# Mixture-of-experts stage: blocks of 64 rows in column halves become blocks of 32 rows in column quarters

## The reference, cut to what matters

```python
def routed_experts(x, expert_ids, gates, wg, wu, wd):
    # assignments sorted by expert, each expert's segment padded to whole blocks
    ...
    def run_block(args):
        tok, gate, e = args
        xb = x_pad[tok]
        hdn = jax.nn.silu(xb @ wg[e]) * (xb @ wu[e])
        return (hdn @ wd[e]) * gate[:, None]
    ...
```

## Time and profile before

| what | value |
|---|---|
| median of 3 runs | 3208.79 us (3207.67 to 3209.72) |
| the profiled execution | 3201.68 us, span 3199.9 us |
| preparation of the experts, 2104 to 2152 | 48 us |
| loop over 82 blocks, 2152 to 3110 | 958 us, 11.66 us per block |
| wait for the last store, 3110 to 3118.3 | 8.3 us |
| tail, 3118.3 to 3200 | 81.7 us |

### The profile page before, as it was taken

The page is one execution under the profiler, slowest core; times in us unless marked ns, Lnnn a source line. Parts: engine busy times, 40 slices in busy tenths (PEclk is TensorE's granted clock), DMA queues, the critical chain, the costliest instruction groups (busy, mean ns, idle before and its releaser), DMA issues. The chain is left out here.

```text
span 3199.9 us, 68748 instructions
## 1 busy us (share of the span) xinstructions
PE 2931.1 (92%) x28939; PEld 1726.0 (54%) x28940; DVE 1408.7 (44%) x3430; ACT 974.0 (30%) x1872; POOL 174.9 (5%) x256
## 2 busy tenths in 40 slices
PE   6988999999999488988898799949999999999988
PEld 2432455454554378878887455535555555555543
DVE  2245356665666545656666344541221211212117
ACT  2357234343344323333333121202122222212215
POOL 0000000000000000000001000001111000111104
PEclk8999999999999799999999799969999999999999
DMA  7541123232233496665552743455896568667758
GB/s 271 208 136 56 50 93 118 93 126 85 100 126 115 132 226 176 179 172 154 154 165 83 233 149 130 165 138 210 306 339 222 180 237 330 253 229 266 261 191 335
DMA packets 373260, 575.69 MB, mean 180 GB/s; under 512 B 31263, under 2 KB 230999, under 8 KB 369977
## 3 DMA queue, kind: packets, MB, share of 16 engines
q1 hardware_dynamic: 332888, 470.13, 43.7%
q0 software_dynamic: 18080, 72.10, 6.4%
q10 hardware_dynamic: 22080, 30.36, 3.3%
HBM read 426.97 MB, written 145.54 MB: 179 GB/s over the span
## 5 line engine op out<-in xcount | busy, mean ns | idle before, releaser
L451 PE MATMUL pj_P<-pj_hT,pj_wc 128*128 128x448 f32 (+2 forms) x1600 | 590.4, 516 | 0.9 <-ACT pj_stage L579 0.9
L2503 PE MATMUL moe_PG<-wgu,moe_xT 128*64 128x256 f32 x5248 | 582.2, 380 | 0.7 <-ACT moe_xT L2401 0.7
L2503 PEld LDWEIGHTS moe_PG<-wgu,moe_xT 128*64 128x64 f32 x5248 | 377.6, 137 | 226.0 <-issue 47.6
L451 PEld LDWEIGHTS pj_P<-pj_hT,pj_wc 128*128 128x128 f32 x1600 | 294.1, 189 | 256.5 <-issue 239.4
L2510 PE MATMUL moe_PTY<-wd,moe_hT 128*64 128x512 f32 x1312 | 317.7, 603 | 0.0
L2404 ACT ACT_TABLE_LOAD x82 | 105.2, 1283 | 496.9 <-issue 496.8
L1984 PE MATMUL merge_PO<-merge_w,merge_mT 128*128 128x512 f32 x544 | 238.5, 596 | 0.0
L2363 DVE TENSOR_TENSOR moe_sg<-moe_sg,moe_PG 128x128 f32<-128x128 f32 x164 | 46.3, 282 | 296.5 <-ACT moe_sg L2404 296.5
L1984 PEld LDWEIGHTS merge_PO<-merge_w,merge_mT 128*128 128x128 f32 x544 | 102.4, 191 | 123.1 <-issue 122.4
L2367 DVE COPY moe_hT<-moe_PH 128x128 f32<-128x128 f32 x164 | 47.9, 292 | 267.2 <-PE moe_PH L2495 267.2
L2370 DVE COPY moe_y<-moe_PTY 128x512 f32<-128x512 f32 x82 | 56.7, 692 | 208.3 <-PE moe_PTY L2510 208.3
(11 more groups left out here) (385 smaller groups left out, 4133.4 us busy)
## 6 DMA issues: line engine op xcount, KB each, us to landing
wgu<-in_w_gate SPq DMA_DIRECT2D x32, 2048.0 KB, 9.4
wgu<-in_w_up SPq DMA_DIRECT2D x32, 2048.0 KB, 15.0
wd<-in_w_down SPq DMA_DIRECT2D x32, 2048.0 KB, 16.6
re_hkf<-scratch_hk SPq DMA_DIRECT2D x60, 640.0 KB, 8.1
re_rkf<-scratch_rk SPq DMA_DIRECT2D x68, 320.0 KB, 6.9
scratch_hk<-pj_hk SPq DMA_DIRECT2D x16, 1344.0 KB, 5.8
scratch_y_rows<-moe_y ACTq DMA_DIRECT2D x164, 128.0 KB, 5.2
scratch_rk<-pj_rk SPq DMA_DIRECT2D x16, 1120.0 KB, 4.4
```

Of the source, the lines that this page charges most:

```text
L451: ins = eng.matmul(bank[:, 0:wp], wc[:, j, k, :], hT[:, k, k0:k0 + wp], start=(k == 0), stop=(k == KD - 1), skip_group_check=True)
L2503: ins = eng.matmul(PG[64 * c:64 * c + 64, j, 0:256].rearrange("p (a b) -> p a b", a=2), x_rows, wgu[p][:, :, k, o:o + 128], start=(k == 0) ...
```

## The change

- `BLOCK` is 32. An expert has at least two blocks. The block's rows are gathered as four quarters of 1 KB into `xg[p]` [128, 256] (two buffers); POOL copies `xg[p]` to `xc`, from which PE makes two transposes instead of four.
- gate_up uses four column quarters of the array, 32 stationary columns each: 32 matmuls of 256 columns. down uses four quarters as well: 16 matmuls of 256 columns.
- PE's order in a step g is `turn(g + 1)`, `turn_hid(g - 1)`, `gate_up(g)`, `down(g)`, and `down(g)` computes the result of block g - 1. It needs `hT_kept >= g` and `y_kept >= g + 1`.
- In DVE's iteration g the copy to `y` (`keep_y(g + 1)`) stands ahead of the copy to `hT`. It waits for `down(g)` and for `y_out`, that is, for the landing of the store of the step before.
- The stores move from the ACT queue to SP's, four DMAs of 32 KB, in a loop per expert, between the loads of weights: at the end of an expert gate and up of the expert after next are issued; then, in the next expert, first one store, then w_down, then the other stores.
- ACT preloads the sigmoid's table once, ahead of the loop.
- Zeros are stored to all of `y_rows` in `merge`, three DMAs of 512 KB per tile on SP's queue; ACT's loop of such stores is gone, and results are stored one block further down.
- In the preparation two scans replace the 17 additions of `carry`, and the block map has 201 columns instead of 101.
- The loads of `maps` come after the last store of a result, since that is now ahead of them on SP.

```diff
-BLOCK = 64
-MAX_BLOCKS = T * TOP_K // BLOCK + N_EXPERTS
+BLOCK = 32
+MIN_BLOCKS = 2
+MAX_BLOCKS = T * TOP_K // BLOCK + MIN_BLOCKS * N_EXPERTS
...
(merge, SP, after the store of h2)
+                for part in range(3):
+                    eng.dma_start(t["y_rows"][ds(at_tile(i, n) * 3 + 128 * part, 128), :], zeros[:, :]).then_inc(ev("zeros_out"), 16)
...
(experts, SP)
-                def load_pair(i):
-                    before, first, second = blocks_of_pair(eng, i - 1)
-                    for p in range(2):
-                        done = before + first if p == 0 else before + first + second
-                        eng.wait_ge(ev("gu_made"), done)
-                        load_expert(eng, t, i * 2 + p, wgu[p], wd[p], loaded[p], range(2))
-                        eng.wait_ge(ev("y_made"), done)
-                        load_expert(eng, t, i * 2 + p, wgu[p], wd[p], loaded[p], range(2, 3))
+                def store_y(g):
+                    eng.wait_ge(ev("y_kept"), g + 2)
+                    ...
+                    for n in range(4):
+                        eng.dma_start(t["y_rows"][ds(at * BLOCK, BLOCK), 256 * n:256 * n + 256], y[32 * n:32 * n + 32, :]).then_inc(ev("y_out"), 16)
+                def expert_blocks(g0, count, down_of, gate_up_of):
+                    store_y(g0)
+                    if down_of is not None:
+                        e, p = down_of
+                        load_expert(eng, t, e, wgu[p], wd[p], loaded[p], range(2, 3))
+                    with eng.Fori(1, count) as b:
+                        store_y(g0 + b)
+                    if gate_up_of is not None:
+                        e, p = gate_up_of
+                        eng.wait_ge(ev("gu_made"), g0 + count)
+                        load_expert(eng, t, e, wgu[p], wd[p], loaded[p], range(2))
+                def pair(i):
+                    before, first, second = blocks_of_pair(eng, i)
+                    expert_blocks(before, first, (i * 2 + 1, 1), (i * 2 + 2, 0))
+                    expert_blocks(before + first, second, (i * 2 + 2, 0), (i * 2 + 3, 1))
...
+                store_y(total(eng))
                 eng.wait_ge(ev("rows_made"), 1)
                 eng.dma_start(maps[:, 0, :], ...
...
(experts, DVE)
-                for n in range(NT):
-                    src = ...
-                    step(eng.tensor_tensor(carry[:, n + 1, :], carry[:, n, :], src, ALU.add))
+                    step(eng.tensor_tensor_scan(carry[:, experts_of, :]..., restart[:, experts_of, :]..., PTY[:, h, 0:n], 0.0, ALU.mult, ALU.add))
...
+                def keep_y(g):
+                    eng.wait_ge(ev("y_made"), g)
+                    eng.wait_ge(ev("y_out"), g * 64)
                     eng.tensor_copy(y[:, :], PY[:, :]).then_inc(ev("y_kept"), 1)
+                with eng.Fori(0, n_blocks) as g:
+                    eng.wait_ge(ev("sigmoid_made"), g + 1)
+                    eng.tensor_tensor(sg[:, :], sg[:, :], PG[:, 0, 0:128], ALU.mult).then_inc(ev("silu_made"), 1)
+                    eng.wait_ge(ev("silu_made"), g + 1)
+                    eng.tensor_tensor(hid[:, :], sg[:, :], PG[:, 0, 128:256], ALU.mult).then_inc(ev("hid_ready"), 1)
+                    keep_y(g + 1)
+                    eng.wait_ge(ev("h_turned"), g + 1)
+                    eng.tensor_copy(hT[:, :], PH[:, 0, 0:128]).then_inc(ev("hT_kept"), 1)
...
(experts, ACT)
+                eng.preload_act_table_set("sigmoid_and_others")
-                with eng.Fori(total(eng), MAX_BLOCKS + 1) as g:
-                    eng.dma_start(t["y_rows"][ds(g * BLOCK, BLOCK), :], zeros[:, :]).then_inc(ev("row_blocks"), 16)
-                    for n in range(2):
-                        eng.dma_start(t["y_rows"][ds(g * BLOCK, BLOCK), 512 * n:512 * n + 512], y[64 * n:64 * n + 64, :]).then_inc(ev("y_out"), 16)
...
(experts, POOL)
+                        eng.tensor_copy(row[:, p:p + 1], rows[:, ds(i * 2 + (p + 2), 1)]).then_inc(ev("row_ready"), 1)
+                        eng.wait_ge(ev("x_turned"), i * 2 + (p + 1))
+                        eng.tensor_copy(xc[:, :], xg[p][:, :]).then_inc(ev("x_moved"), 1)
+                        ...
+                        gather(p)
...
(experts, PE)
+                def gate_up(g, p):
+                    eng.wait_ge(ev("xT_kept"), g + 1)
                     for k in range(KD):
+                        x_rows = xT[:, k % 2, 32 * (k // 2):32 * (k // 2) + 32]
+                        for q in range(4):
+                            ins = eng.matmul(PG[32 * q:32 * q + 32, 0, 0:256].rearrange("p (a b) -> p a b", a=2), x_rows, wgu[p][:, :, k, 128 * q:128 * q + 128],
                                              start=(k == 0), stop=(k == KD - 1))
+                def down(g, p):
+                    eng.wait_ge(ev("hT_kept"), g)
+                    eng.wait_ge(ev("y_kept"), g + 1)
+                    for k in range(KE):
+                        for n in range(4):
+                            ins = eng.matmul(PY[32 * n:32 * n + 32, :], hT[:, 32 * k:32 * k + 32], wd[p][:, k, 256 * n:256 * n + 256],
+                                             start=(k == 0), stop=(k == KE - 1))
+                def rest_of_expert(g0, count, p):
+                    with eng.Fori(1, count) as b:
+                        g = g0 + b
+                        turn(g + 1)
+                        turn_hid(g - 1)
+                        gate_up(g, p)
+                        down(g, p)
```

More of the change, by code:

```diff
@@ L2211, in experts @@
         x1 = sb("x1", [128, N_KEPT, D])
[L2212 to L2219, removed]
+        quarter = sb("quarter", [128, 1])
+        restart = sb("restart", [128, N_EXPERTS, NT])
+        xg = [sb(f"xg{p}", [128, 256]) for p in range(2)]
+        xc = sb("xc", [128, 256])
+        xT = sb("xT", [128, 2, 128])
+        sg = sb("sg", [128, 128])
+        hid = sb("hid", [128, 128])
+        hT = sb("hT", [128, 128])
+        y = sb("y", [128, 256])
         PTY = ctx.enter_context(nc.psum_tensor("moe_PTY", [128, 2, 512], F32))
@@ L2266, in _ @@
                 with eng.Fori(1, 1 + N_KEPT) as i:
-                    load_pair(i)
+                    pair(i)
                     eng.dma_start(x1[:, ds(i - 1, 1), :].rearrange("p a n -> p (a n)"), t["x1"][ds(i * 128 - 128, 128), :]).then_inc(ev("x1_in"), 16)
-                with eng.Fori(1 + N_KEPT, N_EXPERTS // 2) as i:
-                    load_pair(i)
+                with eng.Fori(1 + N_KEPT, N_EXPERTS // 2 - 1) as i:
+                    pair(i)
+                before, first, second = blocks_of_pair(eng, N_EXPERTS // 2 - 1)
@@ L2271, in _ @@
+                expert_blocks(before, first, (N_EXPERTS - 1, 1), None)
+                expert_blocks(before + first, second, None, None)
+                store_y(total(eng))
                 eng.wait_ge(ev("rows_made"), 1)
@@ L2497, in gate_up, with turn, turn_hid @@
-                def gate_up(p, j):
+                def turn(g, first=False):
+                    eng.wait_ge(ev("x_moved"), g + 1)
+                    if not first:
+                        eng.wait_ge(ev("xT_kept"), g)
+                    for k in range(2):
+                        ins = eng.transpose(PT[:, k, :], xc[:, 128 * k:128 * k + 128], ident)
+                    ins.then_inc(ev("x_turned"), 1)
+                def turn_hid(g):
+                    eng.wait_ge(ev("hid_ready"), g + 1)
+                    eng.transpose(PH[:, 0, 0:128], hid[:, :], ident).then_inc(ev("h_turned"), 1)
@@ L2504, in gate_up @@
                                              start=(k == 0), stop=(k == KD - 1))
-                    ins.then_inc(ev("g_made" if j == 0 else "gu_made"), 1)
-                def down(p, j, c):
-                    for n in range(2):
-                        ins = eng.matmul(PY[64 * n:64 * n + 64, :], hT[:, j, 64 * c:64 * c + 64], wd[p][:, 2 * c + j, 512 * n:512 * n + 512],
-                                         start=(j == 0 and c == 0), stop=(j == 1 and c == 1))
-                    return ins
@@ new lines, in rest_of_expert, with next_expert @@
+                def rest_of_expert(g0, count, p):
[5 more added lines that the diff above has]
+                        down(g, p)
+                        eng.nop()
+                def next_expert(g, i, p):
+                    turn(g + 1)
+                    turn_hid(g - 1)
+                    for matrix in range(2):
+                        eng.wait_ge(loaded[p][matrix], i * 16 + 16)
+                    eng.sem_inc(ev("expert_begun"), 1)
+                    gate_up(g, p)
+                    down(g, 1 - p)
+                    eng.wait_ge(loaded[p][2], i * 16 + 16)
+                    eng.sem_inc(ev("down_begun"), 1)
@@ new lines, in _ @@
+                turn(0, first=True)
+                before, first, second = blocks_of_pair(eng, 0)
+                for matrix in range(3):
+                    eng.wait_ge(loaded[0][matrix], 16)
+                eng.wait_ge(ev("xT_kept"), 1)
+                turn(1)
+                gate_up(before, 0)
```

(9 more changed lines are left out.)

169 lines of the change are left out of this document (80 added, 89 removed).

## The result

The changed kernel takes 3323.17 us (median of four runs, 3316.77 to 3329.83), beside 3209.26 us for the kernel before on the same chip: a ratio of 1.035, interval 1.033 to 1.037. The forecast was 3262, with a range up to 3320. The direction was right, and the loss is twice as large as forecast.

A forecast was written before the change was run, and what follows sets the result against it. PE was taken to bound the loop: 885 of work, 94 of store stalls and 27 of clock make 1006 (+48); with +5 outside the loop, 3255 us profiled, 3262 in the median's scale. Range 3150 to 3320.

The forecast's parts named there:

- PE bounds the loop, a step is near half, the blocks are 150: Loop: PE's step falls from 11.66 to 5.89 us, 82 blocks become 150; 885 us, 73 less than 958.
- Stores go to the end of SP's queue and PE waits in the third step of every expert: Expert boundaries: the store lands behind gate and up at D + 17.1 (D: last down's end), so PE's down waits; 0.72.
- The size of the wait: Loop: PE stalls 2.1 us at a plain boundary, longer with x1 or handed-on lateness; 94 us over 30 boundaries.
- the same walk: Going through the 30 expert boundaries with the row counts: 14 stalls of 2.1, 11 of about 3.5, four of 5.0, one of 6.4.
- The clock: Loop: PE's granted clock falls after idle time, 1.7 us lost at each of 16 stalls of 3.4 us and more; 27 us.
- upper cases: Loop, more waits than forecast: the table load stays (+22) and loads pass at 380 GB/s (+33), 3317 us; chance 0.05.
- Not held up, 3141: Rival, loop: stores pass queued loads or loads finish in time, no stall or clock loss, -68 us; chance 0.11.
- Quarters in series, 3970: Rival, PE's matmuls: the column quarters don't run side by side, a step of 11.1 us, about +710; chance 0.01.
- Parts forecast at nothing: ACT's table load gone, POOL's copy hidden, weights never late, zeros in merge 0 (up to +5 at the last tile).

The follow-up runs named there:

- Experiment 1: The changed kernel with its four y stores per block issued on ACT's queue instead of SP's: 3211.3 us, 1.002 of the kernel before.
- experiment 6: The changed kernel with the load of w_up moved behind the store of the next expert's first step, ahead of w_down: 3340.37 us, 1.041 of the kernel before.
- experiment 9: The changed kernel with weight loads on ACT's queue, stores alone on SP's, x1 ahead of the loop: 3179.11 us with one y tile, then (last kernel) 3129.99 with two.
- 4: The changed kernel with the twelve x1 tiles loaded ahead of the loop, on SP's queue behind the constants: 3303.36 us, 1.032 of the kernel before.

## Why the prediction was right or wrong

- **PE bounds the loop, a step is near half, the blocks are 150.** Right: 5.80 us against 5.89, 13 us better over the loop. The quarters run side by side.
- **Stores go to the end of SP's queue and PE waits in the third step of every expert.** Right, all 30. Experiment 1 took the waits away by the queue, experiment 6 moved them by the order in the queue. With x1 ahead in both, separate queues gave 3179 against 3303 (experiments 9 and 4), 124 us (what SP gains in not issuing loads is in it). The Trainium skill (DMA: Bandwidth & Descriptors, section "Issuing engines are not separate DMA queues") says that starting DMAs from several engines only saves issuing time; these runs differ from it, and the prediction was right not to follow it. That section also says that the DMAs of all engines interleave on the same 16 DMA engines. The trace agrees as far as a store on its own queue still took 6.3 us under the loads, and 47 us hang on that.
- **The size of the wait: 94 forecast, 139 measured by the same walk** (134.8 in the view of waits). This is the step that failed by most microseconds. At a plain boundary the walk has 3.5 us (3.35 in the view) against 2.1. Three terms make the difference. Gate left at D + 3.5 and not D + 3.1. PE was ready at D + 15.6 and not D + 15.9, since its steps were shorter. And the passage of the bytes was met to a tenth (gate and up through 13.7 us after gate's issue, the store 14.05), but DVE's copy began only 0.8 to 1.0 us after the store's last packet, at every boundary, where I had put 0.1: the time from a last packet to its landing was missing from the sum. With x1 the view has 5.4 against a forecast of 3.4. There SP is held 4.23 us in issuing x1 and the store of G is issued only at D + 10.6, but that isn't what made it late. In all twelve its first packet ran 14.2 to 14.8 us after gate's issue, at least 7.1 after its own, and without x1 12.9 to 13.2 after gate's. So x1's place in the queue costs 1.4 us, as forecast, and the store's own packets are under way for 1.8 us instead of some 1.2.
- **The clock: 27 forecast, some 53 to 58 measured.** This is the step that failed most for its size. I charged 1.7 us to the 16 waits of 3.4 us and more, from a single row of 2.25 us idle. Nearly every wait turned out at 3.2 or more, and 28 brought the half clock, at about 2 us each; two of 3.38 and 3.41 us did not. The 58 are what is left of 197 beside the 139; some 5 of them are small gaps, since the last kernel of experiment 9, without waits or falls, has an excess of 5. Of -13 for the steps, +45 for the waits and +31 for the clock the sum is +63, which is the loop's error (1069.6 against 1006).
- **The range.** Its upper cases were taken one at a time. A longer passage lengthens the wait and lets more waits reach the clock, so the two errors go together; 3317 to 3320 had no room for that.
- **Not held up, 3141.** Even off the loads' queue one y tile gives 3179 (experiment 9): a landing of 5.2 to 6.8 us was harmless beside a step of 11.66 and is not beside 5.80. That rival was priced too low by this.
- **Quarters in series, 3970.** The sum of this rival is off: its 710 are over the kernel before, and were added to 3262, which holds the waits already. It should have been some 3930. Nothing else hangs on it.
- **Parts forecast at nothing.** Right: with the zeros PE is busy for 268.91 us of the 280 in merge (267.37 in the earlier trace rows), the DMA share is up from 0.48 to 0.70, and merge's own length grows by 0.4 us; no table load is left in the loop; POOL's copy is waited for only ahead of the first block; no expert's weights come late. From merge's last matmul to the first gate_up it is 54.0 us against 51.8, +2.2 where the forecast had some +4; the tail is +1.6 against +1.5. The 3.0 us ahead of merge belong to no term of the sum.

## What to carry to other kernels

When a change shortens a step, set every hand-off's landing time against the new step, not against its bytes: the same queue that cost nothing at 11.66 us per step cost 112 to 124 us at 5.80. Keep small stores with a waiter off the queue of the bulk loads, and give their tile a second buffer; here, with x1 moved in all three, the first alone left 52 us of 198, the second alone 23, both together 5. Add to a DMA's passage the time from its last packet to its landing, here 0.8 us. Of 30 idle stretches of PE of 3.2 to 6.5 us, 28 cost about 2 us of clock on top of their length.

## What the runs showed of the hardware that was not expected

- One store DMA of 128 KB in four pieces landed later (8.9 us) than four of 32 KB (6.3), with 132 packets for 192, and with at most 4 of them under way at once instead of up to 9. Fewer issues are not fewer microseconds.
- Code volume reached PE in the middle of a DMA-heavy loop: with copied steps, 14 waits of 6.2 to 7.3 us appeared at the pair loop's ends, each with a 16 KB instruction fetch inside it, and they went when a filling was written with less code.
- An engine can be held while it issues behind loads that are still under way: SP 4.23 us with one x1 tile behind two loads, 3.37 us with four small stores instead of 1.82. Neither delayed the bytes, whose turn in the queue came later still.
- Behind an idle stretch of 3.35 us PE was granted 0.58 over the next 4 us, and its down took 3.53 us instead of 1.91.
